# Attention heads in pairs, wider VectorE operations, and constant products on TensorE around two norms and the router, in a two-layer hybrid decoder

## What is computed

```python
def rms_norm(x, g):
    y = x * lax.rsqrt(jnp.mean(x * x, axis=-1, keepdims=True) + EPS)
    return y * g
def modulate(x, g, shift, scale):
    return rms_norm(x, g) * (1 + scale[:, None, :]) + shift[:, None, :]

def swa_sink_attention(h, w_q, q_norm, sinks, w_o, k_win, v_win, mask, cos, sin):
    q = rotary(rms_norm((h @ w_q).reshape(bsz, seq, 16, 64), q_norm), cos, sin)
    # per block of 128 queries, its own 128 keys and the 128 before; 4 key heads, 4 query heads each
    s = jnp.einsum('bqkgd,bskd->bkgqs', qi, ki) * HEAD_DIM ** -0.5
    s = jnp.where(mask, s, -jnp.inf)
    p = jax.nn.softmax(jnp.concatenate([s, sink_col], axis=-1), axis=-1)[..., :-1]
    return o(einsum('bkgqs,bskd->bqkgd', p, vi)) @ w_o

def moe_swiglu(h, w_router, w_gu, w_down):
    top_v, top_i = lax.top_k(h @ w_router, 2)
    top_w = jax.nn.softmax(top_v, axis=-1)
    # out = sum over 8 experts of gate * ((silu(h @ w_g) * (h @ w_u)) @ w_down), width 3584
```

## Time and profile before

| | |
|---|---|
| median of 3 runs | 1540.36 us (1538.50 to 1540.86) |
| the profiled execution | 1540.05 us; its span, first to last instruction, 1538.3 us |
| busy, of the span | TensorE 96%, VectorE 84%, ScalarE 64%, GpSimd 4% |
| mean granted TensorE clock | 0.969 of full speed |
| DMA | 485 MB, mean 316 GB/s |
| norm 2 to the end of the K/V projection | 380 to 410 us |
| query projections | 410 to 448 us |
| attention | 448.5 to 500.2 us |
| output projection, norm 3, router | 500.2 to 563.4 us |
| experts | 563.4 us to the end |

### The profile page before, as it was taken

One profiled execution on the slowest core, in us unless ns is written; L12 is line 12 of the kernel. 1 busy time (PEld: TensorE's weight loads), 2 busy tenths in 40 slices (PEclk: granted clock), 3 DMA queues, 4 the chain that ended last, 5 costly groups with the idle time before them and its releaser, 6 DMA issues.

```text
span 1538.3 us, 18990 instructions
## 1 busy us (share of the span) xinstructions
PE 1479.6 (96%) x7456; PEld 1228.1 (80%) x7457; DVE 1288.1 (84%) x1539; ACT 992.0 (64%) x1193; POOL 62.9 (4%) x57
## 2 busy tenths in 40 slices
PE   7998999999889989999999999999999999999996
PEld 3887899999445878888888888888888888888885
DVE  5786998987568449799999999999999999999995
ACT  2252434343336248688888888888888888888884
POOL 0000000000000030001001001001001001000001
PEclk9999999999879969999999999999999999999998
DMA  9986879799530629999999999999999999999970
GB/s 337 325 302 211 307 274 326 276 329 364 183 110 1 219 90 374 329 363 363 393 383 363 393 382 361 394 384 355 397 386 369 389 388 368 379 393 372 375 299 16
DMA packets 222158, 485.44 MB, mean 316 GB/s; under 512 B 6160, under 2 KB 33008, under 8 KB 222064
## 3 DMA queue, kind: packets, MB, share of 16 engines
q1 hardware_dynamic: 217296, 474.04, 84.0%
q0 software_dynamic: 2160, 7.87, 2.0%
q10 hardware_dynamic: 2608, 2.27, 0.4%
HBM read 477.86 MB, written 6.29 MB: 315 GB/s over the span
## 4 chain that ended last, share of the span: by engine, by line
issue 51%; PE 34%; DVE 6%; POOL 3%; SPq 2%; DMA 1%; ACT 1%; ACTq 0%; DVEq 0%; POOLq 0%
PE bank L1547 5%; PE bank L1548 4%; PE bank L1549 4%; PE bank L1741 3%; PE bank L1742 3%; PE bank L1743 3%; PE bank L1452 2%; PE bank L1607 2%; SPq L532 2%; DMA ring<-in_ada_w 1%; PE bank L1472 1%; POOL y L602 1%; POOL out L606 1%; PE bank L1587 1%; DVE sqb L956 1%
## 5 line engine op out<-in xcount | busy, mean ns | idle before, releaser
L1310 DVE TENSOR_TENSOR wlo<-ring,whi 128x1024 fp32r<-128x1024 f32 x672 | 815.0, 1236 | 78.1 <-ACT whi L871 56.8
L871 ACT ACTIVATE whi<-ring 128x1024 fp32r<-128x1024 f32 x672 | 711.6, 1062 | 179.0 <-PE bank L1743 178.8
L1741 PE MATMUL bank<-whi,xh 128*128 128x512 f32 x904 | 360.6, 399 | 4.2 <-DVE wlo L1310 3.8
L1743 PE MATMUL bank<-wlo,xh 128*128 128x512 f32 x904 | 354.7, 392 | 0.0
L1742 PE MATMUL bank<-whi,xl 128*128 128x512 f32 x904 | 354.3, 392 | 0.0
L1741 PEld LDWEIGHTS bank<-whi,xh 128*128 128x128 f32 x904 | 170.9, 189 | 41.3 <-issue 7.8
L1743 PEld LDWEIGHTS bank<-wlo,xh 128*128 128x128 f32 x904 | 170.9, 189 | 36.7
L1742 PEld LDWEIGHTS bank<-whi,xl 128*128 128x128 f32 x904 | 171.2, 189 | 33.8
L1741 PE MATMUL bank<-whi,hh 128*128 128x512 f32 x440 | 172.1, 391 | 0.0
L1743 PE MATMUL bank<-wlo,hh 128*128 128x512 f32 x440 | 171.5, 390 | 0.0
L1742 PE MATMUL bank<-whi,hl 128*128 128x512 f32 x440 | 171.3, 389 | 0.0
(11 more groups left out here) (258 smaller groups left out, 1634.7 us busy)
## 6 DMA issues: line engine op xcount, KB each, us to landing
ring<-in_m_w_gu SPq DMA_DIRECT2D x112, 2048.0 KB, 11.2
ring<-in_m_w_down SPq DMA_DIRECT2D x56, 2048.0 KB, 10.7
ring<-in_ada_w SPq DMA_DIRECT2D x24, 2048.0 KB, 14.5
ring<-in_f_w_gu SPq DMA_DIRECT2D x24, 1024.0 KB, 14.1
ring<-in_f_w_down SPq DMA_DIRECT2D x6, 2048.0 KB, 14.6
ring<-in_a_w_in SPq DMA_DIRECT2D x4, 2048.0 KB, 18.8
ring<-in_kv_ada_w SPq DMA_DIRECT2D x4, 2048.0 KB, 12.3
ring<-in_a_w_out SPq DMA_DIRECT2D x2, 2048.0 KB, 10.4
```

Of the source, the lines that this page charges most:

```text
L871: nc.scalar.activation(whi[:, n % WB, :], moe_raw(n), ACT.Copy).then_inc(hi_ready, 1)
L1310: v_.tensor_tensor(wlo[:, n % WB, :], moe_raw(n), whi[:, n % WB, :].bitcast(F32), ALU.subtract).then_inc(lo_ready, 1)
L1741: mm(o, hi, whi[:, b, c0:c0 + 512], start=start, stop=False)
L1743: return mm(o, hi, wlo[:, b, c0:c0 + 512], start=False, stop=stop)
```

## The change

In attention, a step is a pair of heads (p) in place of a head (h). The PSUM banks become one tensor, so that one instruction can read two of them. The scores of a pair go to two banks, and the two heads' products of equal width are issued one after the other; a step of scores begins with four constant products, and those between the other parts are gone. VectorE scales, masks and takes the maximum in one `tensor_tensor_reduce` for each head and block, with the sink as the start of the maximum and with no wait between the four; the product with the inverse sums goes over both heads at once; the argument of the sink's exponential is made on VectorE. ScalarE takes the sink's exponential for both heads and both blocks in one, and copies the transposed probabilities of a pair in one. The copy of the output moves from ScalarE to VectorE. The probabilities have three buffers of a pair in place of four of a head, and lie partly in `C`; the transposed ones lie in `G`. TensorE runs two pairs of scores ahead.

Elsewhere only constant products are added: 8 ahead of and 16 behind the statistics of norm 2, 12 behind those of norm 3 and its adaLN columns, 18 between the products for the positions and the gather.

```diff
+        score_bank = lambda p, j: bank[2 * (p % 2) + j]
...
+            def exps(p):
+                act.wait_ge(nm_done, p + 1)
+                for j in range(2):
+                    h = 2 * p + j
+                    nc.scalar.activation(Pb[p % 3][:, j, 0:P], Pb[p % 3][:, j, 0:P], ACT.Exp, bias=nm[:, h, 0:1],
+                                         accum_out=sm[:, h, 0:1])
+                    nc.scalar.activation(Pb[p % 3][:, j, P:3 * P], Pb[p % 3][:, j, P:3 * P], ACT.Exp,
+                                         bias=nm[:, h, 1:2], accum_out=sm[:, h, 1:2])
+                act.wait_ge(es_set, p + 1)
+                then(nc.scalar.activation(es[:, 2 * p:2 * p + 2, :], es[:, 2 * p:2 * p + 2, :], ACT.Exp), ex)
+
+            def copy_p(p):
+                act.wait_ge(pT_mm, p + 1)
+                if p >= 2:
+                    act.wait_ge(pv_mm, p - 1)
+                then(nc.scalar.activation(PT[:, 2 * (p % 2):2 * (p % 2) + 2, :], psum[:, 4:6, 0:3 * P], ACT.Copy), pt)
...
+            def scores(p):
+                dve.wait_ge(sc_mm, p + 1)
+                if p >= 3:
+                    dve.wait_ge(pT_mm, p - 2)
+                pair = slice(2 * p, 2 * p + 2)
+                for j in range(2):
+                    h = 2 * p + j
+                    for c0, c1, i in ((0, P, 0), (P, 3 * P, 1)):
+                        ins = v_.tensor_tensor_reduce(out=Pb[p % 3][:, j, c0:c1], in0=score_bank(p, j)[:, c0:c1],
+                                                      in1=mask[:, c0:c1], scale=HD ** -0.5, scalar=sinks[:, h:h + 1],
+                                                      op0=ALU.add, op1=ALU.max, accum_out=mx[:, h, i:i + 1])
+                then(ins, sce)
+                then(v_.tensor_scalar(nm[:, pair, :], mx[:, pair, :], -1.0, None, ALU.mult), nms)
+                then(v_.tensor_tensor(es[:, pair, :], nm[:, pair, :], sinks[:, pair][:, :, None].to_broadcast([P, 2, 2]),
+                                      ALU.add), ess)
...
+            for p in range(2):
+                scores(p)
+            for p in range(NH // 2):
+                probs(p)
+                if p + 2 < NH // 2:
+                    scores(p + 2)
+                if p:
+                    copy_o(p - 1)
+            copy_o(NH // 2 - 1)
...
+            keep_clock(bank[0][:, :], 8)
 
             stats(2)
+            keep_clock(bank[0][:, :], 16)
...
+            def scores(p):
+                if p >= 2:
+                    pe.wait_ge(sc_evac, p - 1)
+                else:
+                    pe.wait_ge(qkT_done, 6)
+                g = 2 * p // (NH // NKV)
+                keep_clock(score_bank(p, 0)[:, :], 4)
+                for j in range(2):
+                    lo = HD * j
+                    mm(score_bank(p, j)[:, 0:P], B[lo:lo + HD, p, 0:P], kT[lo:lo + HD, g, 0:P], start=True, stop=True)
...
+            for p in range(2):
+                scores(p)
+            for p in range(NH // 2):
+                if p + 2 < NH // 2:
+                    scores(p + 2)
+                probs_T(p)
+                if p:
+                    values(p - 1)
+            values(NH // 2 - 1)
...
+            keep_clock(bank[0][:, :], 12)
...
+            keep_clock(bank[0][:, :], 18)
             pe.wait_ge(ht_done, 4)
```

More of the change, by code:

```diff
@@ L251, in build @@
         nm_done = sem("nm_done")
+        es_set = sem("es_set")
         exp_done = sem("exp_done")
@@ L1216, in _ @@
-            for h in range(NH):
-                if h + 2 < NH:
-                    scores(h + 2)
-                probs(h)
+            sce, nms, ess, pns, oe = (Signal(sc_evac), Signal(nm_done), Signal(es_set), Signal(pn_done),
+                                      Signal(o_evac))
+            def scores(p):
[13 more added lines that the diff above has]
+                                      ALU.add), ess)
@@ new lines, in probs @@
+            def probs(p):
+                pair = slice(2 * p, 2 * p + 2)
+                dve.wait_ge(exp_done, p + 1)
+                then(v_.tensor_tensor(sm[:, pair, :], sm[:, pair, :], es[:, pair, :], ALU.add))
+                then(v_.reciprocal(sm[:, pair, :], sm[:, pair, :]))
+                for c0, c1, i in ((0, P, 0), (P, 3 * P, 1)):
+                    ins = v_.tensor_tensor(Pb[p % 3][:, :, c0:c1], Pb[p % 3][:, :, c0:c1],
+                                           sm[:, pair, i:i + 1].to_broadcast([P, 2, c1 - c0]), ALU.mult)
+                then(ins, pns)
@@ L1220, in _, with copy_o @@
+            def copy_o(p):
+                dve.wait_ge(pv_mm, p + 1)
+                then(v_.tensor_copy(A[:, p, :], bank[6 + p % 2][:, 0:SEQ]), oe)
+            for p in range(2):
[7 more added lines that the diff above has]
+            copy_o(NH // 2 - 1)
             dve.wait_ge(qk_tp, 6)
@@ new lines, in scores, with probs_T @@
+                for j in range(2):
+                    lo = HD * j
+                    last = mm(score_bank(p, j)[:, P:3 * P], B[lo:lo + HD, p, P:2 * P], kT[lo:lo + HD, g, :], start=True,
+                              stop=True)
+                last.then_inc(sc_mm, 1)
+            def probs_T(p):
+                pe.wait_ge(pn_done, p + 1)
+                if p:
+                    pe.wait_ge(pT_evac, p)
+                for j in range(2):
+                    for i in range(3):
+                        last = transposed(bank[4 + j][:, i * P:(i + 1) * P], Pb[p % 3][:, j, i * P:(i + 1) * P],
+                                          ident[:, :])
+                last.then_inc(pT_mm, 1)
@@ new lines, in values @@
+            def values(p):
+                pe.wait_ge(pT_evac, p + 1)
+                if p >= 2:
+                    pe.wait_ge(o_evac, p - 1)
+                g = 2 * p // (NH // NKV)
+                v0, v1 = vt[:, 0, g * HD:(g + 1) * HD], vt[:, 1, g * HD:(g + 1) * HD]
+                for j in range(2):
+                    o = bank[6 + p % 2][HD * j:HD * j + HD, :]
+                    p_ = PT[:, 2 * (p % 2) + j, :]
+                    mm(o[:, 0:P], v0, p_[:, 0:P], start=True, stop=True)
+                    mm(o[:, P:2 * P], v0, p_[:, P:2 * P], start=True, stop=False)
+                    last = mm(o[:, P:2 * P], v1, p_[:, 2 * P:3 * P], start=False, stop=True)
+                last.then_inc(pv_mm, 1)
```

95 lines of the change are left out of this document (13 added, 82 removed).

## The result

The changed kernel takes **1522.82 us** (median of 4 runs, 1520.79 to 1526.29) where the kernel before took 1539.43 beside it (4 runs): ratio 0.9901, 95% interval 0.9886 to 0.9915. The two medians differ by 16.6 us; the ratio on record is not their quotient and stands for 15.2. The forecast was 1532.4 with a range from 1526 to 1538: the right direction, and about half of the gain (7.7 us). The profiled execution took 1524.15 us, its span is 1522.4, and the two spans differ by 15.9.

The account below looks back on a forecast made before the run. TensorE, 96% busy, was taken as the bound, losing time where its clock runs low. Norm 2 5.2, attention 1.1 and router 1.4 sum to 7.7 us off 1540.05, 0.3 for the median: 1532.4, range 1526 to 1538.

Parts of the forecast that it names:

- Norm 2, minus 5.2: Norm 2 and K/V projection: constant products hold the clock, statistics end 2.7 us earlier, projection gains 2.8; 5.2 taken.
- Attention, minus 1.1: Attention: 50.7 us for 51.7 before; most of the gain per head is given back in a longer low-clock start.
- the sum of TensorE's pair: Attention at full clock: constants 0.87, shape change 0.1, scores 1.5, transposes 0.75, values 1.5; together 4.7 us, making TensorE the bound.
- The rival with the overlap of the scores: Attention: a pair's scores run at once on two row halves, minus 4.5 us in all, 1528; chance 25%.
- The evidence against it: Values of heads 14 and 15: the second starts 0.21 us after the first's last, read as column halves not overlapping.
- VectorE's pair, 4.45: Attention: VectorE's work per pair takes 4.45 us for 5.48 before (low 3.9, high 6.0), reductions 2.0 of it.
- the loop: Attention: output copy, probabilities, transposes and values wait on each other, 4.4 us a round, close under TensorE's 4.7.
- The clock in attention: Start of attention: low clock at first, rising 17.5 us after the start, where before it rose after 15.0.
- The twelve products, 0: Router: twelve constant products end 0.3 us after its first operand is ready; its first half catches up, 0.
- The eighteen, minus 1.4: Router: gather starts 2.0 us later but takes 3.4 for 6.6, minus 3.2; with 0.2 regained in the experts, minus 1.4.
- the experts' start: Experts' first 5.9 us: of the 3.0 us lost there to the low clock, 0.2 counted as regained.
- the walk: Attention summed round by round: low-clock start 17.4 (17.5 taken), 3.7, four rounds 18.8, last rounds 10.7; 50.7 us.

Follow-up runs that it names:

- before_both_waits: The kernel before, with head 14's values held until head 15's transposed probabilities are there too: 1536.42 us (one execution), both heads' values done in 1.15 us.
- changed_again: The changed kernel, unaltered, run again on a second chip: 1519.53 us, ratio 0.9891, with the kernel before at 1536.97 beside it.
- no_18: The changed kernel without the 18 constant products behind the router's scores, ahead of the gather: 1521.99 us, ratio 0.9899.
- the separate parts: Changed kernel without the 8, 16, 12 and 18 constant products: 1529.18 us, ratio 0.9947; kernel before with only those added: 1532.76, ratio 0.9964.

## Why the prediction was wrong, point by point

- **Norm 2, minus 5.2: right.** 5.6 in the trace; no run has these 24 products alone. The projection started at 390.33 for 390.45 predicted, at full clock.
- **Attention, minus 1.1: wrong, it was 8.0, and this is the miss.** The step of the prediction that failed is the sum of TensorE's pair, 4.7 us with scores of 1.5 and values of 1.5, and from it "TensorE is the bound". Scores are 0.9 and values 1.07, since the two heads' products run at once, in the row halves and in the column halves. The price of a pair on TensorE is 3.8 with its constants. Taking the overlap away brings the rounds back to 5.4 and the time to 1541. That is also above what the prediction forecast for products that run one after the other: without the added product a round is 5.2 and not 4.7 (scores 1.7 for 1.5, values 1.6 for 1.5, and a little more for constants and transposes), and the time would be 7 to 10 us above the forecast 1532.4 (by the median and by the ratio, less 1.7 for the added products). Two errors of opposite sign stood in the sum, and the larger was the missing overlap. The rival with the overlap of the scores (25%, 1528) had the mechanism, but only in the scores, with the values one after the other. On the Trainium skill's page "TensorE: Matmul & The Clock Gate", Part 3, row and column tiles run at once; the trace after shows both.
- **The evidence against it** was one pair of rows whose gap had another cause, shown by before_both_waits. It was looked up on TensorE alone. The copy that released head 15 is in ScalarE's rows of the same trace.
- **VectorE's pair, 4.45: too high.** 3.77. The reductions cost 1.45, not 2.0, near the low bound: I had added 0.14 to each for its read, and the reads lie beside the next reduction. So neither engine was as full as forecast, and the loop, forecast at 4.4, became the bound at 4.0, with values of 1.07 in it. The loop's parts and order were right.
- **The clock in attention: wrong.** Forecast back 17.5 us after the start, it came back after 4.6 (442.95 to 447.5), but fell twice more, for 3.5 and 6.5 us. With both kinds of products apart it came back after 17.8, with the scores alone apart after 27.3: the forecast is near what a kernel without the overlap does, and missed what the overlap changed. That the low time in all, 14.5 us, is near the forecast is luck. From the start of attention to the output projection it was low for 15.0 us before and for 14.5 in the changed kernel: in this profile the gain doesn't come from the clock. In changed_again it is low for two stretches only, and attention takes 1.8 us less.
- **The twelve products, 0: right** (the router's first product starts 0.2 later, and nothing measurable changes without them). **The eighteen, minus 1.4: right in this profile** (gather 2.0 later, 5.8 us of constants, 2.9 us won in the gather), and the experts' start gave back 1.4, not 0.2, since its clock was low for 3.5 us instead of 5.9. But no_18 shows no loss that can be measured without the 18, so part of what I credited to them may belong to the clock's place.
- **The range.** Its lower end, 1526, was the overlap in the scores plus what the experts may add. It held neither the overlap of the values nor cheaper reductions together with it. Errors of one sign in terms that feed the same loop add up. Two slips of 0.1 us in the walk (4 x 0.43 and 2 x 1.59 make 4.9, not 4.8; 51.7 less 50.7 is 1.0, not 1.1) change nothing.

What stays open: why the constants in attention don't raise the share of full clock while the stretch with those of norm 2 has it, why the clock came back sooner where the scores overlap, and the split of the last 1 to 2 us between the parts. The sum of the separate parts (13.7 us by ratio) and the whole (15.2 and 16.8 on two chips) agree within their intervals, which is all they can say.

## What to carry to other kernels

Before a row is used as evidence that two instructions don't overlap, check that the second one's operand was there when the first ran: look at every engine that feeds it. Two edits that lighten two engines of one loop are to be priced together; here neither alone gave more than 3 us, and both gave 8. And when a copy out of PSUM stands in an engine's order ahead of the work that its partner waits for, move it one round later: it was worth some 4 us here.

## What the runs showed that I had not expected

Products on different row halves (64 x 128 operands) and on different column halves run at once when they stand next to each other: four scores products in 0.9 us for 0.85 of two, six values products in 1.07 for 0.80 of three; a full-width product between them costs its own 0.21 us and the whole overlap, another 0.53 (values). An accumulator read on VectorE (0.08 us) costs no time of its own between two such reductions. And the clock's level over a stretch of attention differs between two profiles of one and the same program (20.5 and 10.2 us low between 430 us and its end), with 2 us of attention behind it.
